# Two layers of a mixer and expert block: one written order for the work ahead of the experts, and inverse roots from a logarithm and an exponent

## The reference

```
mod = silu(c) @ ada_w[l] + ada_b[l]            # six vectors: shift, scale, gate, twice; the same for c_ctx
h  = rms_norm(x, norm1_g) * (1 + sc1) + sh1    # x and, in layer 0, the context too
p  = h @ w_in                                  # groups A (gating), B (Fourier), C and D (attention)
y  = merge(gating(A), fft(B), diff_attention(C), neighbourhood_attention(D))
                                               # merge: rms norm of each head of 64, times a gain, @ w_out
x  = x + g1 * y
x  = x + g2 * expert_choice_ffn(rms_norm(x, norm2_g) * (1 + sc2) + sh2)
# the expert part: softmax over 16 experts, each takes its 32 best tokens; gate, up and down matrices of 1024 x 1024
```

## Time and profile before

| | us |
|---|---|
| median of three runs | 3208.1 (3206.53 to 3215.99) |
| the profiled execution | 3215.48 |
| its span, first to last instruction | 3213.7 |
| front part of layer 0, up to the first expert matmul | 0 to 479 |
| experts of layer 0 | 479 to about 955 |
| front part of layer 1 with the sums ahead of it | about 955 to 1288.5 |
| experts of layer 1 | 1288.5 to about 1765 |
| second half | about 1765 to 3214 |

### The profile page before, as it was taken

One profiled execution on the slowest core, in us unless ns is written; L12 is line 12 of the kernel. 1 busy time (PEld: TensorE's weight loads), 2 busy tenths in 40 slices (PEclk: granted clock), 3 DMA queues, 4 the chain that ended last, 5 costly groups with the idle time before them and its releaser, 6 DMA issues.

```text
span 3213.7 us, 31872 instructions
## 1 busy us (share of the span) xinstructions
PE 2920.2 (91%) x12556; PEld 1673.7 (52%) x12556; DVE 915.2 (28%) x1842; ACT 548.0 (17%) x1053; POOL 92.1 (3%) x160
## 2 busy tenths in 40 slices
PE   6997689888889987999899999999999999999997
PEld 3454434333335544333333776674884866674873
DVE  2545431111114453111101524343101525343001
ACT  1143311111111241111110212220000213310000
POOL 3000000000001000000000100001000000000000
PEclk9997689999999987998888999999999999999999
...
GB/s 290 119 39 134 53 81 409 409 410 410 410 405 196 118 138 131 382 409 410 410 410 407 150 138 98 79 79 159 133 149 150 131 131 84 100 92 140 139 148 59
DMA packets 237054, 669.75 MB, mean 208 GB/s; under 512 B 8016, under 2 KB 18568, under 8 KB 236944
## 3 DMA queue, kind: packets, MB, share of 16 engines
...
## 4 chain that ended last, share of the span: by engine, by line
PE 75%; DMA 17%; DVE 5%; issue 2%; ACT 1%; POOL 0%; SPq 0%; DVEq 0%; ACTq 0%; POOLq 0%
PE bank L737 31%; DMA ring<-in_exp_w_up_dram 16%; PE bank L750 9%; PE bank L1262 9%; PE bank L1280 5%; PE bank L1123 4%; PE bank L950 3%; PE bank L302 3%; PE bank L1146 1%; PE bank L1085 1%; PE bank L890 1%; PE bank L1001 1%; PE bank L791 1%; PE bank L912 1%; PE bank L988 1%
## 5 line engine op out<-in xcount | busy, mean ns | idle before, releaser
L750 PE MATMUL bank<-ring,arena 128*64 128x512 f32 (+1 forms) x3072 | 720.5, 623 | 112.8 <-DMA ring<-in_exp_w_up_dram 63.5
L737 PE MATMUL bank<-arena,ring 128*128 128x256 f32 x2432 | 529.1, 379 | 0.0
L750 PEld LDWEIGHTS bank<-ring,arena 128*64 128x64 f32 (+1 forms) x3072 | 219.4, 128 | 588.2 <-issue 478.7
L737 PEld LDWEIGHTS bank<-arena,ring 128*128 128x128 f32 x2432 | 461.1, 190 | 67.3
L737 PE MATMUL bank<-ring,arena 128*128 128x512 f32 (+1 forms) x1120 | 469.7, 580 | 1.7 <-DVE arena L2658 1.7
L737 PEld LDWEIGHTS bank<-ring,arena 128*128 128x128 f32 x1120 | 211.7, 190 | 250.9 <-issue 246.2
L1262 PE MATMUL bank<-ring,arena 128*128 128x512 f32 x640 | 297.5, 596 | 0.0
L302 PE MATMUL bank<-arena 128*128 128x128 f32 (+4 forms) x516 | 86.2, 320 | 121.2 <-DVE arena L2174 45.1
L1280 PEld LDWEIGHTS bank<-ring 128*128 128x128 f32 x1248 | 154.0, 192 | 42.0 <-issue 37.3
L2344 DVE COPY arena<-bank 128x512 f32<-128x512 f32 (+1 forms) x64 | 44.0, 688 | 450.9 <-PE bank L750 450.9
L1262 PEld LDWEIGHTS bank<-ring,arena 128*128 128x128 f32 x640 | 112.8, 192 | 94.0 <-issue 94.0
...
## 6 DMA issues: line engine op xcount, KB each, us to landing
...
```

Of the source, the lines that this page charges most:

```text
L737: last = mm(o, lhs(k), rhs(k), start=start and k == 0, stop=stop and k == kt - 1)
L750: last = mm(U(us[c])[g * rows:(g + 1) * rows, :], lhs(k), rhs(i, c), start=(k < 2), stop=(k >= KT - 2))
```

## The change

1. `fill`, `fill_table`, `mix` and `before_experts` are gone. Each stage is a program of its own: `a4` to `a11` (a modulation product and its fold), `A0`.. and `B0`.. (projections), `F0`.. (Fourier), `g0`.. (gating), `o0`.. (output tile), `R0`.. and `G0`.. (route and gather of a stream), `r0`, `r1` (rows of the gates). `follow` steps them in the order of a written plan per layer. A "/" in the plan is a step of attention (`J`). A stage's chain across engines is cut into more steps, so that steps of others can stand between: `o` has 21.
2. The projections A2, A3 and the gatings g2, g3 stand between steps of the first two output tiles, `R0` beside attention, `G0` between steps of the last output tile, `ada` 10 and 11 beside `R1` (layer 0) or the last output tile (layer 1).
3. Chunks of the front part are loaded in the order of PRE_ORDER into the slots of PRE_PLACE. In layer 0 chunks `a7`, `a8`, `a9` and `a10` use one slot. The load of `a8` waits for twelve counted chunks, and the twelfth is `a7`. A used chunk is counted by `let_go` at the next matmul that calls it; matmuls of attention and of the folds don't.
4. An inverse root is exp(-0.5 * ln(mean)) on ACT (`ac_inverse_roots`), then one Newton step of three small DVE instructions (`refined`). The mean with its epsilon is one DVE instruction ahead (`mean`). The gating norms, one root for all tiles before, have one per tile.
5. The second norm of the output tile waits for ACT's square sum on DVE (`square_sum`, `x_stat`).

The rows below are the instructions of one engine in order, by line, operation and shape.

The diff, cut to its core:

```diff
+PRE_ORDER = [
+    "a0 a1 a2 a3 CQ DQ V a4 a5 A B a6 a7 w0 w1 a8 a9 a10 a11".split(),
+    "a0 a1 a2 a3 CQ DQ V a4 a5 A B a6 a7 a8 w0 w1 a9 a10 a11".split()]
+PRE_PLACE = [(0, 1, 2, 3, 0, 1, 2, 3, 0, 1, 2, 3, 0, 2, 3, 0, 0, 0, 1),
+             (0, 1, 2, 3, 0, 1, 2, 3, 0, 1, 2, 3, 0, 1, 2, 3, 0, 1, 0)]
 PRE_CHUNKS = 19
...
+    """a4 a4 / a4 / a5 a5 / a5 a4 / A0 A0 / a4 a5 A0 / a5 A0 / A0 r0 / A1 A1 g0 / A1 A1 g0 / A1 r0 g0 / r0 B0 B0 g1 /
+    B0 g0 g1 / g0 B1 B1 g1 / B1 g1 / g1 B2 B2 / B2 B3 B3 / B3 F0 F0 / F0 F1 / F1 / F1 F0 / F0 F0 / F1 F1 / F1 a6 a6 /
+    o0 a6 a7 a7 / o0 o0 a7 a6 / a6 a7 / a7 o0 / o0 a8 a8 / a8 o0 o0 / o0 o0 a8 / a8 o0 o0 / o0 o0 / o0 a9 a9 /
+    o0 o0 a9 A2 A2 / a9 A2 A2 / a9 A2 o0 / o0 / o0 / o0 o0 A3 A3 /
+    o1 A3 A3 / o1 o1 A3 g2 / o1 g2 g3 / o1 g2 g3 / g2 o1 o1 g3 / g2 o1 o1 / g3 o1 o1 / g3 o1 o1 / o1 / o1 o1 / o1 /
+    o1 / o1 / o1 o1 / R0 / R0 / R0 o2 / R0 o2 o2 / o2 / o2 / o2 o2 / o2 o2 / o2 o2 / o2 / o2 / o2""",
...
+    """o3 G0 G0 o2 o2 o3 o3 G0 G0 o2 o2 o2 o3 o2 o2 o3 o3 o3 o3 o3 o3 o3 o3 o3 o3 G0 G0 o3 o3 G0 G0 o3 o3 G0 o3 o3 o3
+    R1 a10 a10 a10 R1 a11 a11 a11 a10 G0 R1 a10 a11 a11 r1 r1 r1 R1 G1 G1 G1 G1 G1 G1 G1 G1 G1 G1""",
+    """o1 o0 o0 o1 o1 a10 a10 o0 o0 a10 o1 o1 o1 o1 o1 o1 o1 o1 o1 o1 o1 a11 a11 o1 o1 a11 a10 o1 o1 a10 a11 a11 o1 o1 o1
...
 ALL = tuple(range(BANKS))
 DENSE, RULE, SIDE = (0, 1), (2, 3, 4, 5), (6, 7)
 ARENA = 28632
...
-        def fill_table(l):
...
-            entries = 2 * n + 2
-            until = 31 if l < DEPTH - 1 else 19
-            table = [base * (i + 1) // until - base * i // until for i in range(until)]
-            rest = [1] * (entries - until)
-            if l == DEPTH - 1:
-                rest[-2] = 0
-            return table + rest
...
+        def follow(l, programs):
+            for name in PLAN[l]:
+                next(programs[name], None)
+            for name, program in programs.items():
+                assert next(program, "end") == "end", (l, name)
...
+                def take(name):
+                    s = PRE_SLOTS[l][PRE_PLACE[l][PRE_ORDER[l].index(name)]]
+                    nc.tensor.wait_ge(sem[f"chunk{s}"], pe.due(f"chunk{s}", 16))
+                    return slot[s]
+                def let_go(ins):
+                    if pending[0]:
+                        ins.then_inc(sem["chunk_used"], 1)
+                        pending[0] -= 1
+                def ada(j):
+                    w = take(f"a{j}")
+                    u = rows_of[j] = bank_for(DENSE)
+                    for k in range(KT):
+                        g = k % 4
+                        last = mm(U(u)[32 * g:32 * g + 32, :], m["silu_c"][:, 2 * k:2 * k + 32], w[:, k, :],
+                                  start=(k < 4), stop=(k >= 4))
+                        if k < KT - 1:
+                            let_go(last)
+                        if k == 3:
+                            yield
+                    last.then_inc(full[u % BANKS], 1)
+                    if j == 11:
+                        held[0] = 1
+                    else:
+                        pending[0] += 1
+                    yield
+                    yield
+                    ada_fold(j, DENSE)
+                    yield
+                    yield
...
+                def turned_xn(t):
                     nc.tensor.wait_ge(sem["xn_ready"], pe.due("xn_ready"))
                     turned = []
                     for j in range(2):
                         u = bank_for(DENSE)
                         for k in range(4):
                             last = turn(U(u)[:, k * P:(k + 1) * P], XN[:, t, (4 * j + k) * P:(4 * j + k + 1) * P])
+                            if k < 3:
+                                let_go(last)
                         last.then_inc(full[u % BANKS], 1)
                         turned.append(u)
+                    return turned
...
+                def out_tile(t):
+                    yield
+                    yield
+                    yield
+                    turned = turned_xn(t)
+                    yield
+                    yield
+                    for c in range(2):
+                        if t == 0:
...
+                                evacuated([turned[k // 4]])
+                            last = mm(U(u)[:, :], HT[:, k, t * P:(t + 1) * P], weights[c][:, k, :],
+                                      start=(k == 0), stop=(k == KT - 1))
+                            if k < KT - 1:
+                                let_go(last)
+                            else:
+                                last.then_inc(full[u % BANKS], 1)
+                                if t == tiles(l)[-1]:
+                                    pending[0] += 1
+                            if k % 2:
+                                yield
+                    yield
+                    yield
+                    yield
+                    turned = turned_xn(t)
+                    yield
                     yield
                     u = bank_for(DENSE)
                     for k in range(KT):
                         if k % 4 == 0:
                             evacuated([turned[k // 4]])
                         last = mm(U(u)[:, 0:N_EXP], HT[:, k, t * P:(t + 1) * P], RW[:, k, :], start=(k == 0), stop=(k == KT - 1))
+                        if k < KT - 1:
+                            let_go(last)
...
-                    for j in range(6, 10):
-                        yield from ada(j, DENSE)
-                        if j > 6:
-                            ada_fold(j - 1, DENSE)
-                    ada_fold(9, DENSE)
-                    for t in tiles(l):
-                        yield from out_tile(t)
...
-                def last_ada():
-                    yield from ada(10, DENSE)
...
+                    programs.update({f"F{i}": fourier_of(i), f"R{i}": route(i), f"G{i}": gather(i)})
+                for j in range(4, 12):
+                    programs[f"a{j}"] = ada(j)
+                for i in range(2):
+                    programs[f"r{i}"] = gate_rows(i)
+                follow(l, programs)
+                assert pending[0] == 0 and held[0] == 1
                 chunks[0] = 0
...
-        def ac_roots(src, n_terms):
-            return nc.scalar.activation(src, src, ACT.Sqrt, scale=1.0 / n_terms, bias=EPS)
+        def ac_inverse_roots(mean, root, then="root"):
+            nc.scalar.activation(root, mean, ACT.Ln).then_inc(sem["scalar_step"], 1)
+            nc.scalar.wait_ge(sem["scalar_step"], ac.due("scalar_step"))
+            nc.scalar.activation(root, root, ACT.Exp, scale=-0.5).then_inc(sem[then], 1)
+            nc.scalar.wait_ge(sem[then], ac.due(then))
...
+                def gate(t):
+                    yield
+                    nc.scalar.wait_ge(sem["gate_stat"], ac.due("gate_stat"))
+                    ac_inverse_roots(SS28[:, t, 0:4], ROOT_GATE[t % 2], "gate_root")
+                    yield
+                    yield
...
+                def out_tile(t):
+                    s = t // 2
+                    yield
+                    nc.scalar.wait_ge(sem["stat"], ac.due("stat"))
+                    ac_inverse_roots(SS[:, 16 * t:16 * t + 16], ROOT_O[t % 2])
+                    yield
+                    yield
...
-                    ac_roots(SST[:, t:t + 1], D).then_inc(sem["root"], 1)
-                    nc.scalar.wait_ge(sem["root"], ac.due("root"))
+                    row(XN[:, t, :], X[:, t, :], ACT.Square, "square_sum", accum_out=SST[:, t:t + 1])
+                    nc.scalar.wait_ge(sem["x_stat"], ac.due("x_stat"))
+                    ac_inverse_roots(SST[:, t:t + 1], ROOT_X[:, t:t + 1])
+                    yield
                     yield
                     ac.unit(lane=DENSE)
...
+            def mean(sums, n_terms, then="stat"):
+                step(ts(sums, sums, 1.0 / n_terms, EPS, ALU.mult, ALU.add), then)
+            def refined(mean, root, which="root"):
+                nc.vector.wait_ge(sem[which], dv.due(which))
+                step(stt(mean, root, -0.5, mean, ALU.mult, ALU.mult))
+                step(tt(mean, mean, root, ALU.mult))
+                step(stt(root, mean, 1.5, root, ALU.add, ALU.mult))
...
+                    step(tt(x, x, bc(ROOT_GATE[t % 2], 2, [P, 4, HD]), ALU.mult), "vn_ready")
+                    yield
+                    u = dv.unit(lane=DENSE)
+                    yield
+                    landed(u)
+                    sv = PROJ[:, t, C_K:C_K + 256]
+                    frees(tt(sv.rearrange("p (h w) -> p h w", h=4), U(u)[:, 0:256].rearrange("p (h w) -> p h w", h=4),
+                             bc(COLS[:, 24:28], 2, [P, 4, HD]), ALU.add), u)
+                    step(tt(PROJ[:, t, 0:256], PROJ[:, t, 0:256], sv, ALU.mult))
...
-                        r = SS[:, 16 * t + o // HD:16 * t + o // HD + g]
+                        r = ROOT_O[t % 2][:, o // HD:o // HD + g]
                         step(tt(XN[:, t, o:o + w].rearrange("p (g w) -> p g w", g=g),
...
```

(4 more changed lines are left out.)

653 lines of the change are left out of this document (308 added, 345 removed).

## The result

The changed kernel takes 3245.2 us (median of 4 runs, 3243.11 to 3253.75), the kernel before 3212.05 beside it. The ratio is 1.0108, with a 95% interval of 1.0091 to 1.0126: slower by 1.1%, some 35 us, where 20 us of gain were forecast. The time lies outside the range given. The profiled execution has a span of 3252.0 us.

| | after | before |
|---|---|---|
| up to layer 0's first expert matmul | 509.5 | 478.9 |
| experts of layer 0 | 477.4 | 475.7 |
| front part of layer 1 | 345.5 | 333.9 |
| experts of layer 1 | 476.9 | 478.6 |
| second half | 1442.7 | 1446.6 |

What follows compares the result with a forecast made beforehand. Experts were taken as DMA-bound, the front parts as held by PE's waits and lower clock. Layer 0's stretches, 219 + 93 + 59.5 + 89 = 460.5 against 479, gave -18.5, layer 1 -1.1: 3208.1 to 3188 us, range 3172 to 3200.

Steps and rivals of the forecast that it cites:

- The roots' price: Each root needs two table loads, +2.1 us; mixer chain 9.0 us, second norm's chain 7.4 us.
- Stretch (1): Layer 0 up to the first tile's squares: 36 us less work, ending at 219 instead of 254.
- The lower level: PE's clock at 1.2 instead of 2.4 GHz; its cost in layer 0's front part to fall from 39 to 15 us.
- Stretch (2): Layer 0, on to the second tile's product end: work 79, idle 7, lower clock 3, load wait 4, sum 93 us.
- `a8`'s 4: Layer 0, second stretch: PE's new wait for the load of `a8`, 2.9 to 10.6 us possible, taken as 4.
- Stretches (3) and (4): Layer 0, on to the third tile's product end, 59.5 us, then to the experts, 89 us.
- The gain comes from fewer waits long enough to drop the clock (15 against 39 us): Layer 0's front part: the lower clock to cost 15 us instead of 39, while idle hardly falls.
- Layer 1: Layer 1's front part: PE's waits 22.2 against 26.1 us, less what roots add, sum -1.1 us.
- C: Rival, slower: second tables cost 50 us if all are exposed, against 24 of cover: +26, 3234 us; chance 0.14.
- B: Rival, no change: gating roots, DVE's longer list and `a8` at the median take another 13 us: 3208; chance 0.22.
- `a8`'s 6.6: Layer 0, second stretch: what the load of `a8` adds if it lands at the median time, +6.6 us.
- My idle sum hardly falls: The argument given for no change: PE's idle in layer 0 is 58 us where it was 60.5 + 5.5.

Runs made afterwards that it cites:

- e4_warm: Changed kernel plus 59 extra PE matmuls whose results nothing reads, put in front of PE's waits: 3250.5 us, 1.0129 of the kernel before.
- e12_earlier: Changed kernel with roots of before, `a8` loaded first, row copies ahead of squares, layer 1's old order, third tile's steps earlier: 3197.5 us, 0.9947.
- e10_oldorder_meanless: New form with a list spelling out the old order, roots as in the kernel before, without the mean step: 3228.5 us, 1.0058 of the kernel before.
- e5_oldorder: New form with a list spelling out the old order, Sqrt and reciprocal roots with the mean step: 3236.2 us, 1.0066 of the kernel before.
- e1_sqrt: Changed kernel in its new order, first block's roots by Sqrt and reciprocal again, mean step kept: 3233.5 us, 1.0075 of the kernel before.
- e2_lnexp: Kernel before in its own order, first block's roots by Ln then Exp, four small VectorE steps for the reciprocal: 3244.6 us, 1.0100.

## Why the prediction was wrong, by its own steps

- **The roots' price.** Two loads, 9.0 us for the mixer chain: right, and Ln took what Exp took (0.22 us each). The chain of the second norm was 9.8 us and not 7.4, by attention's steps on VectorE's row. The tables of ScalarE in the stretch from 110 to 510 us, of before and of the changed kernel:

```profile
L1514 ACT ACT_TABLE_LOAD x10 | 12.8, 1283 | 0.2
L1379 ACT ACT_TABLE_LOAD x8 | 10.3, 1283 | 21.6 <-DVE arena L2167 21.5
```

```profile
L1416 ACT ACT_TABLE_LOAD x12 | 15.4, 1283 | 19.2 <-DVE arena L1978 19.2
L1418 ACT ACT_TABLE_LOAD x12 | 15.4, 1283 | 0.2
...
L1553 ACT ACT_TABLE_LOAD x3 | 3.8, 1283 | 0.4 <-DVE arena L2177 0.4
```

  The loads ahead of attention's exponents (L1514, L1553) have fallen from 10 to 3, those in the roots have risen from 8 to 24: two in each of the eight tile roots and in each of four gating roots, where one gating root stood before. Loads that stood beside PE's work have gone, and loads in the chains on which PE waits have come. The Trainium skill, "ScalarE: Activation LUTs", section "Table sets: the hidden batching unit", has one set for logarithm and exponent; the trace has a load ahead of each of the twelve, so the measurement decides.
- **Stretch (1)** ended at 228.2, not 219. PE's work at full level between 110 us and the squares fell from 138.67 * 0.96 = 133 to 112.00 * 0.93 = 104, so by 29 and not by 36. The stages moved as forecast: `a8`, `a9` and three quarters of `a7` (52 records of the product are ahead, 96 were), four folds, A2, A3 and two gatings. Fewer of attention's jobs moved (its records of values are 88 where they were 115), and seven more records of the projections ahead of attention (49 against 42, 3 us) fall behind the 110 us mark, since attention's first score came 2 us later. The lower level costs 2 us more. The piece before:

```profile
110.00:254.00 144.00, 138.67 (x663) 78.49 (x661) 67.51 (x171) 54.82 (x102) 7.42 (x14) 0.96 0.28 98
```

- **Stretch (2)** took 124 us, not 93. Its work at full level is 99.07 * 0.77 = 76, the forecast 79. Idle is 25 instead of 11 (7 and `a8`'s 4): the folds' 7.4 us were in no term, the second tile's scaling has a wait of 4.5 us that A2 and A3 were to cover, and the products with `w_out` wait 2.7 us for the residual (L2296). Router and gates are no longer than forecast. And the lower level costs 23 instead of 3.
- **Stretches (3) and (4)**: idle 22.9 and 24.2, forecast 23 and 24; work 26 and 56, forecast 31.5 and 58; the lower level 14 and 14, forecast 5 and 7.
- **The step that failed** is "The gain comes from fewer waits long enough to drop the clock (15 against 39 us)". It is 51 against 39. The waits became shorter and more (18 with a longest of 11.0 us from 250 us on before, 29 with a longest of 7.2 from 228 on now), and the mean clock stayed at 0.76, over a longer stretch. The forecast let the cost of the lower level fall to less than half while its own idle sum fell by 8 us; no row showed that fewer long waits would do this. 36 us of the miss in layer 0 are this term, 14 idle and 9 the first stretch, less 10 of work counted too high. In e4_warm the higher clock came with empty work and no gain, in e12_earlier it came as idle itself fell (66 to 47 us, the lower level 48 to 39).
- **The new form** was priced at nothing beside its mean steps and gating roots. e10_oldorder_meanless puts it at 0.58% (18 us) with the roots of before, in a list that follows the old order, though not step for step. Gating roots and the residual's place explain part at most. What the rest is stays open. Along the runs, the 1.08% are 0.66% for the form with its mean steps (e5_oldorder), 0.09% for the order, which isn't resolved, and 0.33% for logarithm, exponent and Newton step (e1_sqrt).
- **Layer 1**: forecast -1, measured +11.6. PE's waits there:

```profile
PE bank L792 <- DVE arena L2031: 14.6, 4, 6.6
PE bank L330 <- DVE arena L2313: 6.9, 1, 6.9
PE bank L330 <- DVE arena L2386: 6.6, 1, 6.6
```

  and of the kernel before, its one wait of a fold:

```profile
PE bank L806 <- DVE arena L1959: 2.7, 1, 2.7
```

  The folds' 14.6 us stood in no term; the one of before stands at the layer's start and is 5.1 now. The longest, 6.6, ends at 1247.3: the fold's row copy stands behind the second norm's scaling on VectorE, so PE waits for the same chain as before, through the filling. The ranks' 6.6 had been forecast as 6. By the runs 2 us are the form (336 against 334), 4 the order (340 against 336) and some 6 the roots (345.5 against 339.9).
- **The rivals.** C had the sign and a part of the mechanism, the second table; it came out at +26 and the kernel at +35, and had 0.14. But 24 of the 35 us are there with Sqrt roots too (e1_sqrt), so C's number is near by luck in part. B's sum doesn't come out as written: 3188 and 13 are 3201; 3208 needs `a8`'s 6.6 beside the 13. The chance was set by what lies under the chains, and e2_lnexp shows that the roots' price is 32 us where nothing was put under them: the cover had to win more than that. "My idle sum hardly falls" stood in the text as what speaks for B; it should have moved the forecast itself.
